# Expert rows added straight into the output by scattering DMAs

## What is computed

```python
g_idx = argmax(h @ w_rg + b_rg); g_w = softmax(...)[g_idx]           # one of 4 groups for a token
top_v, top_i = top_k(e_logits of that group (8 experts), 2)          # two experts of this group
combine = g_w * softmax(top_v)                                       # the token's two shares
for each expert e:
    out += (silu(h @ w_gate[e]) * (h @ w_up[e]) * combine[:, e]) @ w_down[e]
x = x + out
```

## Time and profile before

| | us |
|---|---|
| median of three runs | 1390.83 |
| profiled execution, its own time | 1388.89 |
| its span, first to last instruction | 1387.0 |
| TensorE busy | 1302.6 (94%) |
| loop of steps, project(0) to the end of down(23) | 1068.3 to 1363.2 |
| from there to the end (evacuate, scatter, load back, add, store) | 23.8 |

### The profile page before, as it was taken

One profiled execution on the slowest core, in us unless ns is written; L12 is line 12 of the kernel. 1 busy time (PEld: TensorE's weight loads), 2 busy tenths in 40 slices (PEclk: granted clock), 3 DMA queues, 4 the chain that ended last, 5 costly groups with the idle time before them and its releaser, 6 DMA issues.

```text
span 1387.0 us, 18650 instructions
## 1 busy us (share of the span) xinstructions
PE 1302.6 (94%) x7329; PEld 949.9 (68%) x7329; DVE 588.3 (42%) x961; ACT 374.6 (27%) x746; POOL 702.8 (51%) x719
## 2 busy tenths in 40 slices
PE   6999979899999999999999999999994999999992
PEld 5888858787787777888788878888782333433330
DVE  1144262438893572537674577614225111111113
ACT  4211253412333683111315333601121111111110
POOL 6477644567675302767764545775930333333320
PEclk9999999999999999999999999999996999999997
DMA  6523210442232200242211213722382799999955
GB/s 217 155 77 121 89 35 7 123 157 84 69 122 92 92 2 31 92 152 91 92 61 62 77 62 136 303 71 83 104 353 73 274 376 383 380 374 376 376 226 191
DMA packets 85451, 216.36 MB, mean 156 GB/s; under 512 B 23716, under 2 KB 32628, under 8 KB 71796
## 3 DMA queue, kind: packets, MB, share of 16 engines
q1 hardware_dynamic: 62124, 199.22, 39.0%
q0 software_dynamic: 13824, 8.44, 2.1%
q10 hardware_dynamic: 9416, 7.51, 1.6%
HBM read 255.99 MB, written 26.22 MB: 203 GB/s over the span
## 4 chain that ended last, share of the span: by engine, by line
PE 80%; DVE 5%; DMA 4%; POOL 3%; issue 3%; ACT 2%; DVEq 1%; ACTq 0%; POOLq 0%; SPq 0%
PE ps L141 17%; PE ps L143 17%; PE ps L142 17%; PE ps L1086 10%; PE ps L1098 5%; DMA w_gu<-w_up,over_u 2%; PE ps L977 2%; POOL w_lo L1133 2%; PE ps L776 2%; PE ps L1078 1%; PE ps L894 1%; PE ps L902 1%; DMA xg<-rows_scratch,row_u 1%; ACT pr L1262 1%; DMA back<-y_scratch 1%
## 5 line engine op out<-in xcount | busy, mean ns | idle before, releaser
L1133 POOL TENSOR_TENSOR w_lo<-stage,w_hi 128x512 fp32r<-128x512 f32 (+1 forms) x296 | 397.8, 1375 | 11.1 <-issue 0.7
L1130 POOL CAST w_hi<-stage 128x512 fp32r<-128x512 f32 (+1 forms) x296 | 194.2, 699 | 403.3 <-PE ps L143 382.4
L141 PE MATMUL ps<-hi,w_hi 128*128 128x512 f32 (+1 forms) x600 | 234.0, 390 | 1.6 <-DVEq L1625 0.9
L142 PE MATMUL ps<-hi,w_lo 128*128 128x512 f32 (+1 forms) x600 | 231.9, 386 | 0.0
L143 PE MATMUL ps<-lo,w_hi 128*128 128x512 f32 (+1 forms) x600 | 231.9, 386 | 0.0
L141 PE MATMUL ps<-w_hi,hi 128*128 128x512 f32 (+2 forms) x520 | 185.0, 356 | 1.4 <-POOL w_lo L1133 0.8
L143 PE MATMUL ps<-w_lo,hi 128*128 128x512 f32 (+2 forms) x520 | 183.5, 353 | 0.0
L142 PE MATMUL ps<-w_hi,lo 128*128 128x512 f32 (+2 forms) x520 | 183.4, 353 | 0.0
L1086 PE MATMUL ps<-w_gu,xT 128*64 128x512 f32 x768 | 172.4, 602 | 4.6 <-DMA w_gu<-w_up,over_u 3.3
L141 PEld LDWEIGHTS ps<-hi,w_hi 128*128 128x128 f32 x600 | 112.7, 188 | 28.7 <-issue 3.1
L2244 DVE TENSOR_TENSOR xT<-ps,ffn_kp 128x1024 f32<-128x1024 f32 x24 | 29.4, 1225 | 239.5 <-PE ps L1086 147.6
(11 more groups left out here) (443 smaller groups left out, 1716.5 us busy)
## 6 DMA issues: line engine op xcount, KB each, us to landing
stage<-w_in SPq DMA_DIRECT2D x84, 512.0 KB, 4.5
w_gu<-w_gate SPq DMA_DIRECT2D x32, 1024.0 KB, 11.8
w_gu<-w_up SPq DMA_DIRECT2D x32, 1024.0 KB, 14.1
w_dn<-w_down SPq DMA_DIRECT2D x32, 1024.0 KB, 10.5
stage<-w_out SPq DMA_DIRECT2D x16, 512.0 KB, 4.3
stage<-w_ssd_branch SPq DMA_DIRECT2D x16, 512.0 KB, 4.7
stage<-w_in SPq DMA_DIRECT2D x20, 256.0 KB, 3.1
stage<-w_attn_branch SPq DMA_DIRECT2D x8, 512.0 KB, 4.3
```

The costliest lines, as they stand in the source:

```text
L141: pe.matmul(out, x[0], w[0], start=first, stop=False)
L142: pe.matmul(out, x[1], w[0], start=False, stop=False)
L1130: nc.gpsimd.tensor_copy(hi[:, b, k, 0:n], stage[:, b, k, 0:n])
L1133: last = nc.gpsimd.tensor_tensor(lo[:, b, k, 0:n], stage[:, b, k, 0:n], hi[:, b, k, 0:n].bitcast(F32), ALU.subtract)
```

## The change

1. The residual `xres` is stored into the output early (four DMAs of 512 KB on SP, behind the stores of the normed rows). Each scatter becomes an adding DMA straight into the output; nothing is loaded back, and VectorE's eight instructions and the output stores at the end go.
2. `evacuate` multiplies by the slot's share. The shares are brought to their slots by 16 further one-hot matmuls on TensorE at step 1, from tables that VectorE makes at step 0 (`share_c`, `share_o`); `hot_o` is a second buffer so that `hot_r` lives on.
3. A row must not be named twice within a DMA, nor by two adding DMAs in flight. So a pair takes experts of two groups (`expert_of`), pairs at place 0 hold groups 0 and 1, those at place 1 groups 2 and 3. An overflow step may hold two experts of one group: it is scattered in two halves (64 slots each, the other half's indices out of bounds), the second after the first has landed. A scatter waits for the last ones before it that could share rows (`clashes`).
4. The last two steps change places: step 22 is the last overflow pair, step 23 the last ordinary pair. The last `evacuate` is split in two.

```diff
+def place_of(step):
+    return {STEPS - 2: 2, STEPS - 1: 1}.get(step, step % 3)
 def pair_of(step):
-    return PAIRS + step // 3 if step % 3 == 2 else 2 * (step // 3) + step % 3
+    return PAIRS + step // 3 if place_of(step) == 2 else 2 * (step // 3) + place_of(step)
+def expert_of(pair, half):
+    return 16 * (pair % 2) + 8 * half + pair // 2
+def clashes(step):
+    sets = (0, 1) if place_of(step) == 2 else (place_of(step),)
+    return [max(r for r in range(step) if place_of(r) == place) for place in (*sets, 2) if place in map(place_of, range(step))]
+def landed(step):
+    return sum(32 if place_of(s) == 2 else 16 for s in range(step % 3, step + 1, 3))
...
 # SP
+            for t in range(TT):
+                sp.dma_start(out[0, P * t:P * (t + 1), :], xres[:, t, :]).then_inc(x2_out, 16)
...
-            for b in range(3):
-                sp.wait_ge(y_out[b], 16 * (STEPS // 3))
-            for t in range(TT):
-                for k in range(2):
-                    sp.dma_start(back[:, TT * k + t, :], y_dram[...]).then_inc(back_in[t], 16)
-            for t in range(TT):
-                sp.wait_ge(out_ready, t + 1)
-                sp.dma_start(out[0, P * t:P * (t + 1), :], xres[:, t, :]).then_inc(out_done, 16)
-            sp.wait_ge(out_done, 16 * TT)
+            for s in range(STEPS - 3, STEPS):
+                sp.wait_ge(y_out[s % 3], landed(s))
...
 # TensorE, between project(1) and turn_slot(2)
+                if s == 1:
+                    pe.wait_ge(rt_step, 5)
+                    for hot_one, shares, place in ((hot_r, share_c, p_share[:, 0:PAIRS]), (hot_o, share_o, p_share[:, PAIRS:STEPS])):
+                        for i in range(2 * TT):
+                            last = pe.matmul(place, hot_one[:, i, :].bitcast(F32), shares[:, i, :], start=(i == 0), stop=(i == 2 * TT - 1))
+                    last.then_inc(share_made, 1)
...
 # GpSimd
-            def scatter(s):
+            def scatter(s, half=0):
                 q = pair_of(s)
-                pool.wait_ge(y_ready, s + 1)
-                nc.gpsimd.indirect_dma_start(y_dram, ...out_u[:, q:q + 1]..., yg[s % 3][:], None, ...)
+                if half == 0:
+                    pool.wait_ge(y_ready, s + 1 + (s == STEPS - 1))
+                    for r in clashes(s):
+                        pool.wait_ge(y_out[r % 3], landed(r))
+                else:
+                    pool.wait_ge(y_out[s % 3], landed(s) - 16)
+                where = row_u[:, q:q + 1] if q < PAIRS else late_u[:, half, q - PAIRS:q - PAIRS + 1]
+                nc.gpsimd.indirect_dma_start(out[0], bass.IndirectOffsetOnAxis(ap=where, axis=0), yg[s % 3][:], None,
+                                             bounds_check=S - 1, oob_is_err=False, compute_op=ALU.add).then_inc(y_out[s % 3], 16)
...
             overflow(0)
+            pool.wait_ge(x2_out, 16 * TT)
+            pool.wait_ge(rt_step, 5)
             for s in range(STEPS):
                 if s + 3 < STEPS:
                     pool.wait_ge(turned, s + 1)
                     gather(s + 3)
                 if s > 0:
                     if s % 3 == 0:
                         pool.wait_ge(gu_done, s)
                         pool.wait_ge(dn_done, s)
                         overflow(s // 3)
+                    if s > 1 and place_of(s - 2) == 2:
+                        scatter(s - 2, 1)
                     scatter(s - 1)
+            scatter(STEPS - 2, 1)
             scatter(STEPS - 1)
...
 # ScalarE, evacuate
                 A.wait_ge(dn_done, s + 1)
                 if s >= 3:
-                    A.wait_ge(y_out[s % 3], 16 * (s // 3))
-                A.activation(yg[s % 3]..., ps[1][:, 0:2, :], ACT.Copy).then_inc(y_ready, 1)
+                    A.wait_ge(y_out[s % 3], landed(s - 3))
+                if s == 0:
+                    A.wait_ge(slots_ready, 1)
+                A.activation(yg[s % 3]..., ps[1][:, 0:2, :], ACT.Copy, scale=slot_share[:, q:q + 1]).then_inc(y_ready, 1)
...
 # VectorE, behind the overflow table at step 0: late_u, share_c, share_o, then rt_step; at step 1 slot_share
```

More of the change, by code:

```diff
@@ L91, in next_set @@
         return self.k % 2
+def place_of(step):
+    return {STEPS - 2: 2, STEPS - 1: 1}.get(step, step % 3)
 def pair_of(step):
-    return PAIRS + step // 3 if step % 3 == 2 else 2 * (step // 3) + step % 3
+    return PAIRS + step // 3 if place_of(step) == 2 else 2 * (step // 3) + place_of(step)
 def step_of(pair):
-    return 3 * (pair - PAIRS) + 2 if pair >= PAIRS else 3 * (pair // 2) + pair % 2
+    return [pair_of(s) for s in range(STEPS)].index(pair)
+def expert_of(pair, half):
[5 more added lines that the diff above has]
+    return sum(32 if place_of(s) == 2 else 16 for s in range(step % 3, step + 1, 3))
 def query_block(b):
@@ L171, in program @@
         row_u = sb("row_u", [P, STEPS], mybir.dt.uint32)
-        out_u = sb("out_u", [P, STEPS], mybir.dt.uint32)
+        late_u = sb("late_u", [P, 2, OVER_PAIRS], mybir.dt.uint32)
+        late = sb("late", [P, 1])
+        slot_share = sb("slot_share", [P, STEPS])
         over_u = sb("over_u", [P, 2 * OVER_PAIRS], mybir.dt.uint32)
@@ L346, in program @@
         act_turned, actT_ready, dn_done, y_ready = (sem(n) for n in ("act_turned", "actT_ready", "dn_done", "y_ready"))
-        back_in = [sem(f"back_in{t}") for t in range(TT)]
-        out_ready = sem("out_ready")
-        out_done = sem("out_done")
+        x2_out, share_made, dn_half = sem("x2_out"), sem("share_made"), sem("dn_half")
+        slots_ready = sem("slots_ready")
         mT_ready = sem("mT_ready")
@@ L376, in program @@
             (cos[:], d["c_cos"].rearrange("(t p) f -> p t f", p=P)), (sin[:], d["c_sin"].rearrange("(t p) f -> p t f", p=P)),
-            (order[:], d["c_order"]), (iota[:], d["c_iota"]), (token[:], d["c_token"]),
+            (order[:], d["c_order"]), (iota[:], d["c_iota"]), (token[:], d["c_token"]), (late[:], d["c_late"]),
             (ffn_kp[:], d["ffn_norm_2"][0].rearrange("(p k) -> p k", p=P)),
@@ L495, in _ @@
             sp.wait_ge(lo_ready, LO_CHUNKS)
-            for e in range(4):
-                gate_up(e, e)
-                down(e, e)
+            for b in range(4):
+                gate_up(expert_of(b // 2, b % 2), b)
+                down(expert_of(b // 2, b % 2), b)
             for t in range(TT):
@@ L1098, in down @@
                             last = pe.matmul(p_dn[h, c, :], actT[:, f, h], w_dn[b][:, f, 512 * c:512 * (c + 1)], start=(f == 0), stop=(f == 1))
+                    if (s, c) == (STEPS - 1, 0):
+                        last.then_inc(dn_half, 1)
                 last.then_inc(dn_done, 1)
@@ L1112, in _ @@
                     for i in range(2 * TT):
-                        last = pe.matmul(p_over, hot_r[:, i, :], over_c[:, i, :], start=(i == 0), stop=(i == 2 * TT - 1))
+                        last = pe.matmul(p_over, hot_o[:, i, :], over_c[:, i, :], start=(i == 0), stop=(i == 2 * TT - 1))
                     last.then_inc(over_made, 1)
@@ L1601, in _ @@
                 A.activation(actT[:].rearrange("p f n -> p (f n)"), ps[0][:, 1, 0:2 * P], ACT.Copy).then_inc(actT_ready, 1)
-            evacuate(STEPS - 1)
+            s, q = STEPS - 1, pair_of(STEPS - 1)
+            A.wait_ge(y_out[s % 3], landed(s - 3))
+            for c in range(2):
+                if c == 0:
+                    A.wait_ge(dn_half, 1)
+                else:
+                    A.wait_ge(dn_done, STEPS)
+                A.activation(yg[s % 3][:, 512 * c:512 * (c + 1)], ps[1][:, c, :], ACT.Copy, scale=slot_share[:, q:q + 1]).then_inc(y_ready, 1)
         @block.vector
@@ L2186, in _ @@
             V.tensor_tensor(per_pick, hot[:], rowc[:].unsqueeze(1).unsqueeze(1).broadcast_to([P, 2, TT, N_EXP]), ALU.mult)
-            by_pair = hot[:].rearrange("p k t (q o) -> p (k t) q o", o=2)
+            by_pair = hot[:].rearrange("p k t (a o q) -> p (k t) a o q", a=2, o=2)
             pair = rt[:, 4:6].rearrange("p a t n -> p (a t n)")[:, 0:2 * TT * PAIRS].rearrange("p (i q) -> p i q", q=PAIRS)
-            V.tensor_tensor(pair, by_pair[:, :, :, 0], by_pair[:, :, :, 1], ALU.add)
+            V.tensor_tensor(pair.rearrange("p i (q a) -> p i a q", a=2), by_pair[:, :, :, 0, :], by_pair[:, :, :, 1, :], ALU.add)
             V.drain()
@@ L2214, in table @@
             def table(first, n, p):
-                v, tab, back_by = (tabf[:, i, 0:n] for i in range(3))
+                v, tab = (tabf[:, i, 0:n] for i in range(2))
                 V.tensor_copy(v, p)
@@ L2223, in table @@
                 V.drain()
-                V.tensor_copy(out_u[:, first:first + n], tab)
-                V.tensor_tensor(row_u[:, first:first + n], tab, back_by, ALU.add)
+                V.tensor_copy(row_u[:, first:first + n], tab)
                 return V.drain()
@@ L2239, in _ @@
             V.drain()
+            shares = share[:].rearrange("p k t -> p (k t)")
             def rows_slot(s):
@@ L2274, in _ @@
             V.drain()
```

(14 more changed lines are left out.)

30 lines of the change are left out of this document (14 added, 16 removed).

## The result

The kernel after takes 1403.76 us (median of 7, 1398.58 to 1407.61), that of before beside it 1390.83: ratio 1.0083, interval 1.0066 to 1.0099. It is slower; the forecast was 1385.8, faster. One execution of each kernel was profiled.

A forecast was written before the change was run, and what follows sets the result against it. It took TensorE and, nearly level in the expert loop, the weights' DMA as limits. Terms -17.1 + 7.0 + 2.3 + 4.0 + 0 - 1.2 = -5.0 gave span 1382.0, 1385.8 us on the median's footing; range 1379.5 to 1396.

The forecast's parts named there:

- The tail: After the last down: loads, adds and output stores go, a chain of scatters is left; end D+6.7 for D+23.8, -17.1 us.
- The chain of halves: At the end: half 0 lands at D-1.1, half 1 at D+1.8, last scatter starts at D+2.6 (D: last down ends).
- Step 22: Project of step 22 waits for overflow weights still issued after down of step 20, with nothing to hide it: +7.0 us.
- clock +2.3: After the 7 us gap before project of step 22, TensorE runs at a slower clock: +2.3 us, bounds 0 and 4.
- DMA load: In the loop, adding rows load the DMA engines more, so project waits later at overflow steps: +4.0 us.
- At most one such packet more: Queue 0: an adding row reads one more row; 0.9 us a scatter, two scatters in three steps, 1.8 us.
- the 5.4 called an upper bound: Loop: 0.9 us more at each wait, in six overflow steps (5 to 20), 5.4 us at most by rows.
- POOL's waits: Half 1 waits for half 0, the next scatter for half 1, a gather stands behind; claimed cost 0 us.
- The forecast is wrong if L1078 waits in the loop: Sign against the forecast: turn_slot (L1078) was to wait not at all after step 2.
- the rival: POOL becomes the bound through the two halves: turn_slot 3.4 us late six times, +20, 1405.8 us; chance 0.12.
- my cover of 5 us: Gather(14) there by 1221, TensorE wanting it at 1226.4, so POOL's new waits would cost nothing.
- The start: Sixteen small matmuls before turn_slot(2) take 2.1 us, +0.2, but fill a gap after which TensorE slowed, 1.4 back: -1.2 us.

The follow-up runs named there:

- old order: Kernel after without the exchange of the last two steps (step 22 last ordinary pair, step 23 last overflow pair in two halves): 1388.9 us.
- early loads: Overflow pair's gate and up loads not held for down: in the kernel after 1392.2 us, in the kernel before 1386.1, in after with old order too 1386.5.
- one scatter: Kernel after with one adding scatter for an overflow step instead of two halves: 1404.0 us.
- doubled scatter: Kernel before with each scatter of an ordinary pair issued twice, the second a plain one into a spare scratch: 1400.9 us.
- last run: Kernel after with old order and early loads, and the two empty scatters of the last overflow step left out: 1382.8 us.

## Why the prediction was wrong

- *The tail* (-17.1): wrong by 8.2, the largest error together with the loop. I ended the program at the last landing. The price of POOL's drain stood in the trace of before, 8.9 us from 1364.8, and I did not read it: there it was over by 1373.7, long before the last store, and off the path; taking the loads, adds and stores away put it on the path. Here 4.4 of the 8.2 are what is left of it behind the last landing. The last landing took 6.7 us, not 4.1: 2.6. The chain of halves took 3.8 in place of 2.6: 2.7 a landing, not 2.1. The order of it, three scatters behind each other, was right.
- *Step 22* (+7.0, clock +2.3): right. The stretch grew by 8.2 (a wait of 7.2, and 0.9 for a late gather) and the next by 1.6 through the clock. The old order took both away. With this data the exchange buys nothing: the tails are 14.9 and 14.3.
- *DMA load* (+4.0): the mechanism was right and its size wrong, 12.2 in one execution. "At most one such packet more" gives 14.4 us of all 16 engines; queue 0 grew from 2.1% of 1387 to 3.1% of 1406, which is 14.5 (13.4 when its packets are summed one by one). What failed is the next step, that only half of it shows at a wait, and the 5.4 called an upper bound. Waits of project grew by 4.9, gathers' by 1.6, and each of the three over 2 us lost the clock, 5.7 in all, which I counted at step 22 and nowhere else. Without any loss of clock, in the runs with early loads, the loop still stays 8.4 and 7.7 over 212.0. The 12 scatters with rows in that stretch have 64 rows on the mean, and 168 ns more a row over 16 engines is 8.1 us (9.5 by the mean of the packets): nearly all of it came out as waits, not half at most. The rule cited from the Trainium skill ("Collectives: The Full Stack", section "The bandwidth ceiling: the fold count and why AG ≠ RS ≠ AR"), a second read for each adding chunk, fits these runs in time: 2.2% of the engines' time when copying, 3.1% when adding, 2.9% with a plain second scatter. The read itself is not shown: the profile counts the same bytes read from memory adding and copying (251.80 MB).
- *POOL's waits* (0): nearly right in size, wrong by its own sign. "The forecast is wrong if L1078 waits in the loop" came true (L1095 in after): turn_slot waited for its gather at steps 11 (0.54), 17 (1.06) and 23 (0.88), three of the places that the rival names, and in the run without second halves it did not. So my cover of 5 us did not hold, at a price of 1.6 us in the loop. As the cause of the result the rival was the near miss to be misled by: its 1405.8 lies 2 us from the result, its sign in the profile (68.5 us of waiting for halves) is there, but without the halves the time is the same.
- *The start* (-1.2): a matter of luck. The 16 matmuls took two passes each, 3.9 us at full clock and not 2.1; the clock then fell in four of the runs with them (project(0) to project(2) 32.7 to 33.0) and not in four others (29.2 to 29.5). The kernel before shows both too, 29.2 and, in the run with early loads, 32.0. Also 2.1 us before project(0) are no effect of the change: runs of either design start it at 1067.8 to 1071.0.

## What to carry to other kernels

An adding scatter saved the DMA engines no time against scatter, load back and add: queues 0 and 1 together held them 41.1% of 1387.0 us before and 40.8% of 1405.8 after. It moves that time from the end to the scatter. In a stage where weights keep the engines 97% busy nearly all of it turned into waits here, and some of the waits cost TensorE's clock on top; with the engines 80% busy it cost nothing. Before blaming the engine that waits longest, take its wait away: 46 us less waiting on POOL changed nothing. And a program that ends on a POOL DMA pays its drain: look for an engine's drain in the trace before the work that hides it is taken away.

## What the runs showed of the hardware

- An adding scatter takes POOL 1.57 us to issue, a copying one 1.01; a row's packet of 4 KB holds a DMA engine 327 ns when it is added and 159 when it is copied (medians).
- In quiet, from issue to landing: 3.2 us for a copying scatter of some 64 rows, 4.8 for an adding one and 5.9 to 6.7 for those that end a program (five executions), 2.7 for an empty adding one. Why the first differs is open.
- Where a program ends on a POOL DMA, nothing works between the last landing and the end, for 4.1 to 4.5 us when it added (with rows or empty) and 6.4 when it copied. What the drain waits for is open.
- The length of a wait alone did not decide whether TensorE's clock fell. Granted clock over the project behind a wait, among others: 0.81 to 0.83 behind 1.94 us (old order), 2.20 (one scatter), 2.28 and 2.54 (after), 0.72 behind 3.34 (after), 0.70 behind 3.16 (doubled scatter), but 1.00 behind 2.21 (last run) and 2.64 (doubled scatter), as behind the waits of up to 1.3 in the kernel before. Small matmuls back to back (the shares') did not always hold it.
